# Layer norm: variance, root and reciprocal of four token quarters on four quarters of the partitions

## The reference

```
def layer_norm(x, g, b):                     # x: tokens x 1024
    mu = mean(x, axis=-1)
    var = mean(square(x - mu), axis=-1)
    return (x - mu) * rsqrt(var + eps) * g + b
h = layer_norm(ALPHA * h + block(h), g, b)   # feeds the next block's projections
```

## Time and profile before

| | us |
|---|---|
| median of 3 runs (2442.24 to 2443.97) | 2443.31 |
| the profiled execution, whole time | 2443.01 |
| its span, first to last instruction | 2441.1 |
| PE busy in it | 2391.5 |
| DVE busy | 1713.4 |
| ACT busy | 1339.5 |
| mean granted TensorE clock | 0.994 of full speed |

### The profile page before, as it was taken

The page is one execution under the profiler, slowest core; times in us unless marked ns, Lnnn a source line. Parts: engine busy times, 40 slices in busy tenths (PEclk is TensorE's granted clock), DMA queues, the critical chain, the costliest instruction groups (busy, mean ns, idle before and its releaser), DMA issues.

```text
span 2441.1 us, 48177 instructions
## 1 busy us (share of the span) xinstructions
PE 2391.5 (98%) x18842; PEld 2289.4 (94%) x18842; DVE 1713.4 (70%) x2517; ACT 1339.5 (55%) x2355; POOL 90.2 (4%) x101
## 2 busy tenths in 40 slices
PE   9999999999999999999999999999999999999998
PEld 8898999999899999999999997899999999789998
DVE  7788777777888867786766575676566657667665
ACT  6788655644678855563444445554444444555443
POOL 0000000000100000000100010010001001001000
PEclk9999999999999999999999999999999999999999
DMA  7454555455354455545455553345545544434553
GB/s 216 131 159 126 165 164 161 154 170 189 108 153 139 137 156 160 169 155 181 145 181 174 169 160 106 121 144 178 170 147 179 178 163 152 123 124 142 189 181 113
DMA packets 401046, 380.19 MB, mean 156 GB/s; under 512 B 28223, under 2 KB 397037, under 8 KB 400765
## 3 DMA queue, kind: packets, MB, share of 16 engines
q1 hardware_dynamic: 397821, 373.87, 48.0%
q10 hardware_dynamic: 3072, 4.20, 0.7%
HBM read 372.77 MB, written 1.05 MB: 153 GB/s over the span
## 4 chain that ended last, share of the span: by engine, by line
PE 79%; DVE 12%; ACT 3%; DVEq 3%; issue 1%; SPq 1%; DMA 1%; ACTq 0%
PE ps L583 22%; PE ps L585 21%; PE ps L584 21%; DVE scratch L1806 3%; DVE w_lo L1583 3%; DVEq L1805 2%; PE ps L805 2%; PE ps L836 1%; PE ps L837 1%; PE ps L838 1%; ACT scratch L1082 1%; ACT w_hi L1082 1%; PE ps L854 1%; PE ps L612 1%; PE ps L614 1%
## 5 line engine op out<-in xcount | busy, mean ns | idle before, releaser
L1583 DVE TENSOR_TENSOR w_lo<-raw,w_hi 128x1024 fp32r<-128x1024 f32 x664 | 812.0, 1229 | 423.2 <-ACT w_hi L1082 421.8
L583 PE MATMUL ps<-x_hi,w_hi 128*128 128x256 f32 (+1 forms) x3664 | 1056.4, 288 | 4.3 <-DVE w_lo L1583 1.6
L584 PE MATMUL ps<-x_lo,w_hi 128*128 128x256 f32 (+1 forms) x3664 | 1042.6, 285 | 0.0
L585 PE MATMUL ps<-x_hi,w_lo 128*128 128x256 f32 (+1 forms) x3664 | 1039.8, 284 | 0.0
L1082 ACT ACTIVATE w_hi<-raw 128x1024 fp32r<-128x1024 f32 x664 | 697.7, 1056 | 447.5 <-PE ps L585 370.6
L583 PEld LDWEIGHTS ps<-x_hi,w_hi 128*128 128x128 f32 x3664 | 690.8, 189 | 30.8 <-issue 25.3
L584 PEld LDWEIGHTS ps<-x_lo,w_hi 128*128 128x128 f32 x3664 | 692.2, 189 | 2.0
L585 PEld LDWEIGHTS ps<-x_hi,w_lo 128*128 128x128 f32 x3664 | 693.6, 189 | 0.0
L583 PE MATMUL ps<-big_r,w_hi 128*128 128x272 f32 (+1 forms) x832 | 238.9, 287 | 0.0
L585 PE MATMUL ps<-big_r,w_lo 128*128 128x272 f32 (+1 forms) x832 | 238.2, 286 | 0.0
L1082 ACT ACTIVATE scratch<-ps 128x256 f32<-128x256 f32 (+9 forms) x328 | 122.3, 384 | 154.9 <-PE ps L838 63.8
(11 more groups left out here) (302 smaller groups left out, 3063.1 us busy)
## 6 DMA issues: line engine op xcount, KB each, us to landing
raw<-in_w_in SPq DMA_DIRECT2D x184, 512.0 KB, 4.7
raw<-in_ffn_w_up SPq DMA_DIRECT2D x176, 512.0 KB, 4.3
raw<-in_ffn_w_down SPq DMA_DIRECT2D x64, 512.0 KB, 4.2
raw<-in_mix_w_in SPq DMA_DIRECT2D x64, 512.0 KB, 4.6
scratch<-in_w_in SPq DMA_DIRECT2D x40, 512.0 KB, 4.8
raw<-in_w_mem_kv SPq DMA_DIRECT2D x32, 512.0 KB, 4.8
raw<-in_w_br_ssd SPq DMA_DIRECT2D x32, 512.0 KB, 3.8
raw<-in_ffn_w_down SPq DMA_DIRECT2D x32, 384.0 KB, 3.3
```

The lines of the kernel that those rows point to most:

```text
L583: mm(out, wh, xh, start=first, stop=False)
L584: mm(out, wh, xl, start=False, stop=False)
L585: return mm(out, wl, xh, start=False, stop=last)
L1583: tt(w_lo[:, p % PARTS, :, :], raw_at(slot_of(Q, p))[:, :, (p % 2) * P:(p % 2 + 1) * P], wh_f[:, p % PARTS, :, :], ALU.subtract).then_inc( ...
```

## The change

The offset's and the squares' sums are also, or only, taken by quarters of the tokens: `quarter_sums` issues four products with a 128x32 block of the constant, each over n/4 tokens, whose results go to partitions 0 to 31, 32 to 63, 64 to 95 and 96 to 127 of one bank. The squares (`ps[3]`) are taken in this way only; the offset in this way into `ps[2]` and, as before, whole into `ps[4]`. Square, variance, root and reciprocal are then instructions of n/4 columns. Four products with a selection column (a column of the identity, repeated over 128 columns) bring the four quarters back to all partitions, in `ps[2]`, from which `scaled` now reads. The products that nothing reads become 12 before and 10 after the selection. `less_offset(0)` is split in two single tiles, that of tiles 2 and 3 moves behind `scaled(0)`, and the order of `scaled`, `lower` and `less_offset` is another.

```diff
-WARM = 30
+WARM, WARM_SPREAD = 12, 10
 ...
     def off_first(NL, n):
         pe.wait_ge(S["off_summed"], NL + 1)
         mm(ps[4][:, 0:n], const[:, K_MEAN:K_MEAN + P], off_sum[:, 0:n], start=True, stop=False)
+        quarter_sums(2, off_sum[:, 0:n], n, True, False)
+
+    def quarter_sums(bank, x, n, first, last, done=None):
+        q = n // 4
+        for g in range(4):
+            m = mm(ps[bank][32 * g:32 * (g + 1), 0:q], const[:, K_MEAN:K_MEAN + 32], x[:, g * q:(g + 1) * q],
+                   start=first, stop=last, skip_group_check=True)
+            if last:
+                m.then_inc(S[done], 1)
     def square_first(NL, n):
-        mm(ps[3][:, 0:n], const[:, K_MEAN:K_MEAN + P], sq_sum[:, 0, 0:n], start=True, stop=False)
+        quarter_sums(3, sq_sum[:, 0, 0:n], n, True, False)
     def off_part(T, o, n):
         read(T, o)
+        quarter_sums(2, xT[:, o, TOK2 - n:TOK2], n, False, o == KT - 1, "off_rows_done")
         m = mm(ps[4][:, 0:n], const[:, K_MEAN:K_MEAN + P], xT[:, o, TOK2 - n:TOK2], start=False, stop=(o == KT - 1))
     def square_part(NL, o, n):
-        m = mm(ps[3][:, 0:n], const[:, K_MEAN:K_MEAN + P], squares[:, o, 0:n], ...)
+        quarter_sums(3, squares[:, o, 0:n], n, False, o == KT - 1, "var_done")
     def last_sums(T, NL, n):
         ...
         keep_warm(WARM)
+        pe.wait_ge(S["rstd_made"], NL + 1)
+        q = n // 4
+        for g in range(4):
+            mm(ps[2][:, g * q:(g + 1) * q], const[:, K_ID + 32 * g:K_ID + 32 * g + 1].to_broadcast([P, P]), rstd[:, 0:q],
+               start=True, stop=True).then_inc(S["rstd_spread"], 1)
+        keep_warm(WARM_SPREAD)
# ScalarE
-    act.wait_ge(S["off_done"], NL + 1)
-    fn(off2[:, 0:n], ps[4][:, 0:n], ACT.Square).then_inc(S["off_squared"], 1)
+    act.wait_ge(S["off_rows_done"], 4 * (NL + 1))
+    fn(off2[:, 0:q], ps[2][:, 0:q], ACT.Square).then_inc(S["off_squared"], 1)
-    fn(rstd_in[:, 0:n], rstd[:, 0:n], ACT.Sqrt, ...)
+    fn(rstd_in[:, 0:q], rstd[:, 0:q], ACT.Sqrt, ...)
# VectorE
-    stt(xT[:, o, c], xT[:, o, c], params[:, ds(g_col + o, 1)], rstd[:, 0:n], ...)
+    stt(xT[:, o, c], xT[:, o, c], params[:, ds(g_col + o, 1)], ps[2][:, 0:n], ...)
     v.wait_ge(S["off_squared"], NL + 1)
-    less_offset(0)
-    v.wait_ge(S["var_done"], NL + 1)
-    tt(rstd[:, 0:n], ps[3][:, 0:n], off2[:, 0:n], ALU.subtract).then_inc(S["var_ready"], 1)
-    less_offset(2)
+    v.wait_ge(S["var_done"], 4 * (NL + 1))
+    tt(rstd[:, 0:q], ps[3][:, 0:q], off2[:, 0:q], ALU.subtract).then_inc(S["var_ready"], 1)
+    v.wait_ge(S["off_done"], NL + 1)
+    less_offset(0, 1)
     v.wait_ge(S["rstd_ready"], NL + 1)
-    v.reciprocal(rstd[:, 0:n], rstd_in[:, 0:n])
+    v.reciprocal(rstd[:, 0:q], rstd_in[:, 0:q]).then_inc(S["rstd_made"], 1)
+    less_offset(1, 1)
     v.drain()
+    v.wait_ge(S["rstd_spread"], 4 * (NL + 1))
     if final:
-        for o in range(4):
+        scaled(0)
+        less_offset(2)
+        v.drain()
+        for o in range(1, 4):
             scaled(o)
         less_offset(4)
         ...
     scaled(0)
+    less_offset(2)
     scaled(1)
+    lower(0)
+    lower(1)
+    scaled(2)
     less_offset(4)
-    lower(0)
-    scaled(2)
-    lower(1)
     scaled(3)
     lower(2)
+    lower(3)
+    scaled(4)
     less_offset(6)
-    scaled(4)
-    lower(3)
     scaled(5)
     lower(4)
+    lower(5)
     scaled(6)
-    lower(5)
     scaled(7)
     lower(6)
     lower(7)
```

More of the change, by code:

```diff
@@ L351, in build @@
                  "cturned cT_ready cpv_done cross_ready "
-                 "y_hi_ready y_split branch_part merged_sum merged_hi merged_ready mean_done centred x_summed off_summed sq_summed sq_ready off_done off_squared var_done var_ready rstd_ready ln_scaled bias_ready x_full "
+                 "y_hi_ready y_split branch_part merged_sum merged_hi merged_ready mean_done centred x_summed off_summed sq_summed sq_ready off_done off_rows_done off_squared var_done var_ready rstd_ready rstd_made rstd_spread ln_scaled bias_ready x_full "
                  "ff_tanh h_hi_ready h_ready down_part mla_weights conv2_made mla_hi lat_squared lsum_done lvar_ready lrs_ready lat_ready "
@@ L645, in square_part @@
                 pe.wait_ge(S["sq_ready"], NL * 6 + o - 1)
-                m = mm(ps[3][:, 0:n], const[:, K_MEAN:K_MEAN + P], squares[:, o, 0:n], start=False, stop=(o == KT - 1))
-                if o == KT - 1:
-                    m.then_inc(S["var_done"], 1)
+                quarter_sums(3, squares[:, o, 0:n], n, False, o == KT - 1, "var_done")
             def keep_warm(count):
@@ L1121, in layer_norm @@
                 c = slice(TOK2 - n, TOK2)
-                act.wait_ge(S["off_done"], NL + 1)
-                fn(off2[:, 0:n], ps[4][:, 0:n], ACT.Square).then_inc(S["off_squared"], 1)
+                q = n // 4
+                act.wait_ge(S["off_rows_done"], 4 * (NL + 1))
+                fn(off2[:, 0:q], ps[2][:, 0:q], ACT.Square).then_inc(S["off_squared"], 1)
                 act.wait_ge(S["var_ready"], NL + 1)
-                fn(rstd_in[:, 0:n], rstd[:, 0:n], ACT.Sqrt, bias=const[:, K_EPS + eps:K_EPS + eps + 1]).then_inc(S["rstd_ready"], 1)
+                fn(rstd_in[:, 0:q], rstd[:, 0:q], ACT.Sqrt, bias=const[:, K_EPS + eps:K_EPS + eps + 1]).then_inc(S["rstd_ready"], 1)
                 if final:
@@ L1701, in layer_norm, with less_offset @@
                 c = slice(TOK2 - n, TOK2)
-                def less_offset(o):
-                    t = xT[:, o:o + 2, c]
-                    tt(t, t, wide(ps[4][:, 0:n], 2), ALU.subtract)
+                q = n // 4
+                def less_offset(o, k=2):
+                    t = xT[:, o:o + k, c]
+                    tt(t, t, wide(ps[4][:, 0:n], k), ALU.subtract)
                 def scaled(o):
-                    stt(xT[:, o, c], xT[:, o, c], params[:, ds(g_col + o, 1)], rstd[:, 0:n], ALU.mult,
+                    stt(xT[:, o, c], xT[:, o, c], params[:, ds(g_col + o, 1)], ps[2][:, 0:n], ALU.mult,
                         ALU.mult).then_inc(S["ln_scaled"], 1)
```

## The result

The changed kernel takes 2449.06 us (median of 12 runs, 2444.67 to 2450.48), the one before in the same comparison 2442.96 us (12 runs). The ratio is 1.0023, with a 95% interval of 1.0015 to 1.0031: slower, by some 6 us, inside the range forecast, but about twice the +3.2 us of the sum.

A forecast was written before the change was run, and what follows sets the result against it. PE, busy 98% of the span, was taken to bound the kernel. Gains until the variance and from there to s, less 0.93 us lost behind s, summed over eight norms to +3.2 us: 2446.5 us, range 2440 to 2457.

The forecast's parts named there:

- the range forecast: Whole kernel: 2440 to 2457 us, from the free order to most of the serial quarters and the clock.
- the +3.2 us of the sum: Whole kernel: +0.53 in norms 0, 1, 6, +0.35 in norms 2 to 5, +0.26 in norm 7.
- Until the variance: Norm's sums on PE until the variance starts: gain 0.12 us in norm 0, 0.18 in norm 2.
- The serial quarters, the first rival: Quarter sets: four products one after the other, 0.43 a set, +13 us; chance 0.14, shared with much dearer layout changes.
- From the variance to s: From variance to s, the start of scaled(0): 2.56 us, a gain of 0.28 at 256 columns, 0.40 at 272.
- the warm products decide and not the reciprocal: Ahead of the selection: PE's 12 products that nothing reads set its start, at variance + 1.46 us.
- Behind s: After scaled(0) starts: DVE's new order takes 2.47 us a pair of tiles, first_three ends 0.93 us later against s.
- the end, where +0.26 was forecast: Norm 7, without lower: its last tile waits for all of DVE's list, one double less_offset more; +0.26 us.
- PE being at 98%, all of it counts: Whole kernel: PE is busy 98% of the span, so the norms' summed +3.2 us adds fully to the time.
- The likeliest case: Whole kernel: 2446.5 us, own range 2442 to 2451, counted as the same, granted clock 1.00 in all norms; chance 0.50.
- The clock: Rival: granted clock falls in a norm as small products replace dense ones; +7 us for one norm, 2458 for three; chance 0.14.

The follow-up runs named there:

- e7: e4 with the last whole offset product behind the squares' last quarter set and 7 products that nothing reads in place of 12; 2435.73 us.
- e2: The kernel before with only VectorE's new order, no quarter sums and no selection; 2454.90 us.
- e8: The changed kernel with the double less_offset of tiles 2 and 3 in the wait for the selection, its pairs of lower kept; 2442.55 us.
- e6: The kernel before with one VectorE instruction of 512 columns that changes nothing ahead of last_split in each norm; 2448.79 us.
- e3: The changed kernel with last_split moved from the norm's end to ahead of the wait for the selection; 2449.23 us.
- e4: The changed kernel with VectorE's old order, the double less_offset in the selection wait, and last_split ahead of the last two lower; 2439.72 us.
- e10: The kernel before with an added VectorE instruction of 256 columns that changes nothing ahead of last_split; 2446.59 us.
- e1: The changed kernel with VectorE's old order put back and the double less_offset of tiles 2 and 3 in the selection wait; 2440.38 us.

## Why the prediction was right, and where its sum was not

**Until the variance.** Right in kind, too small in size. Forecast a gain of 0.12 and 0.18 us, measured 0.28 (3.43 to 3.15) and 0.29 (3.56 to 3.27). A set took 0.12 and not 0.15, and a change of layout some 0.15 and not 0.17 (estimate: the squares' last set ends at about 603.81, 2.74 after the start; less three whole products at 0.43 and six sets at 0.12 that leaves 0.73 for five changes). The serial quarters, the first rival, are ruled out: four tiles of 32 columns start side by side. By the Trainium skill, TensorE: Matmul & The Clock Gate, Part 3, semaphore increments by each of a set's products come one behind the other at some 26 ns. The trace agrees in direction: the variance starts 0.21 after the last record of the squares' quarter set ends (603.69 + 0.32 to 604.22), while the selection, whose products come 0.2 apart, is followed within 0.04 (605.47 + 1.10 to 606.61). The difference, 0.17, is more than three further increments at that price (0.08, an estimate from the page's figure), and nothing here says what the rest is. In the sum the variance started 0.25 after the last set's turn, and it was 0.41 (603.81 to 604.22): there the sum was too small, and ahead of it too large (3.04 forecast to the end of the last set, 2.74 measured).

**From the variance to s.** Forecast 2.56 us, measured 2.39 (2.43 at 272 columns), gains of 0.45 and 0.53. The step that was off is "the warm products decide and not the reciprocal". The reciprocal ends at 605.41 and the selection starts 0.06 later, in all eight norms; in norm 2 of e7 it is 0.06 too (1407.50 to 1407.56), though TensorE had stood idle for 0.19 us. So the reciprocal decides, and the 12 warm products only just end in time. The selection starts 1.25 after the variance and not 1.46 (the prediction's own terms, -0.25 + 0.17 + 1.51, make 1.43): the warm products began 0.28 ahead of the variance and not 0.08.

**Behind s.** Forecast 0.93 us, measured 0.81 at 256 columns and 0.71 at 272, but 0.48 in norm 1, which took 9.01 us before and had a wait of its own. The mechanism is the one given: 2.44 us for a pair of tiles, DVE's 0.18 of idle in each. e2 shows it alone, e8 divides it: 0.60 for the double `less_offset`, 0.21 for the pairs (0.62 and 0.08 in norm 2).

**The sum of the norms** was therefore not +3.2 but about -0.5 us (-0.56 in seven norms, +0.08 at the end, where +0.26 was forecast). By itself this part of the change is neutral: VectorE's order takes back what the shorter chain gives.

**What failed is a step that was missing.** "PE being at 98%, all of it counts" took the norm's delay as the only cost. `last_split` stayed at the end of DVE's list, and I never asked what its lateness triggers. It is the buffer's last reader; in norm 2 its end was 0.90 us ahead of TensorE's last product and is now 0.20, which is 0.7 us less for a load with little slack, and TensorE waited 0.97 us where it had not. Behind the six norms that makes +4.5 us in one execution and +6.4 in the other. e6 makes this loss with nothing else of the change in it; in e3, e4 and e7, which keep the quarter sums and have the low weights sooner, it is gone. So the forecast came near by luck, through two errors of opposite sign: the norms 3.7 us too high, the loads behind them 4.5 to 6.4 too low. The likeliest case, a change below 0.2%, is just missed by the ratio of 1.0023, whose interval begins at 1.0015.

**The clock.** In the changed kernel's two executions the granted clock was 1.00 in all eight norms, as the likeliest case said. Between the norms 1 to 7 there was one fall, to 0.50 behind norm 4 after 2.33 us of waiting, in one of the two. What it costs in a median isn't settled.

**Left open.** The stretch behind norm 0 took 574.2 to 580.0 us in twelve executions of eleven kernels, with falls of the clock at different places. What makes e3's median 2 us longer than its profiled execution, and what fills the difference between -0.5 + 4.5 and the measured 6, may lie in it or in slow loads; no run here separates them.

## What to carry to other kernels

When the order of an engine's list changes, look at its last instruction too: what it frees, which transfer starts then, and how far ahead of the bounding engine's need this stands. Measure that distance against the bounding engine and not in time; a faster chain shortens it as a slower list does (e8). And put subtractions that nobody waits for into the idle time that the change itself makes: the same quarters with the old order and the sums first are 7 us faster than before, and as written were 6 slower.

## What the runs showed of the hardware that was not expected

Four float32 products of 64 columns with 128x32 weights, whose results go to different quarters of the partitions, took 0.12 us together, about the 0.11 that one of them alone should take (an estimate, a quarter of the whole product's 0.43). The low weights' subtraction (128x1024) took 1.22 us when it began just before POOL's additions and 1.63 to 1.67 us when it began 0.1 to 0.4 us behind their start, in all norms 0 to 6 of e6 and e10. One load of the same weights at the same place in the program, the last ahead of norm 1 that ACT waits for, took 7.1 and 7.5 us from issue to landing in e1 and e7 and 4.4 to 5.5 us in the other ten executions.
